# Feed-forward gate and up products with both activation parts in one moving operand

## What is computed

```python
D_FF = ((8 * D_MODEL // 3 + 255) // 256) * 256      # 2816
h = rms_norm(x, w) * (1.0 + scale) + shift
y = (silu(h @ w_gate) * (h @ w_up)) @ w_down        # (256,1024) -> (256,2816) -> (256,1024)
```

## Time and profile before

| | |
|---|---|
| three runs, us | 1251.65, 1252.40, 1252.68; median 1252.4 |
| profiled execution: span, us | 1253.3 (the page gives no other time for it) |
| TensorE busy | 1159.8 us, 93%, 8358 matmuls |
| weight loads busy | 1050.5 us, 84% |
| DVE busy | 932.8 us, 74% |
| ACT busy | 589.0 us, 47% |
| GpSimd busy | 74.6 us, 6% |
| chain that ended last | PE 71%, DVE 17%, ACT 5%, DMA 5% |

### The profile page before, as it was taken

One profiled execution on the slowest core, in us unless ns is written; L12 is line 12 of the kernel. 1 busy time (PEld: TensorE's weight loads), 2 busy tenths in 40 slices (PEclk: granted clock), 3 DMA queues, 4 the chain that ended last, 5 costly groups with the idle time before them and its releaser, 6 DMA issues.

```text
span 1253.3 us, 19977 instructions
## 1 busy us (share of the span) xinstructions
PE 1159.8 (93%) x8358; PEld 1050.5 (84%) x8358; DVE 932.8 (74%) x1630; ACT 589.0 (47%) x968; POOL 74.6 (6%) x106
## 2 busy tenths in 40 slices
PE   2798888999998998899999989999989989999996
PEld 1677568899897996799999979999979967999996
DVE  5967868888786976788978688886765867765445
ACT  1534665344355457544444564444443355444433
POOL 0000000000000000097000000000000000000000
PEclk8799899999999999999999999999999998999998
DMA  9991434788884771467889537789722552765730
GB/s 375 360 371 51 172 135 159 306 310 320 273 333 163 298 263 45 151 249 288 307 229 361 212 139 299 301 246 334 275 103 102 110 177 89 267 240 196 185 133 34
DMA packets 40810, 280.83 MB, mean 224 GB/s; under 512 B 4736, under 2 KB 5264, under 8 KB 7952
## 3 DMA queue, kind: packets, MB, share of 16 engines
q1 hardware_dynamic: 37296, 269.27, 59.3%
q0 software_dynamic: 2416, 7.92, 2.1%
q10 hardware_dynamic: 1008, 2.37, 0.6%
HBM read 277.91 MB, written 1.10 MB: 223 GB/s over the span
## 4 chain that ended last, share of the span: by engine, by line
PE 71%; DVE 17%; ACT 5%; DMA 5%; issue 1%; SPq 0%; DVEq 0%; ACTq 0%
PE PS L408 70%; DVE LO L1385 5%; DMA raw<-WS 4%; DVE raw L1375 4%; ACT HI L957 2%; DMA SC<-scratch 1%; DVE TMP L1485 1%; DVE TMP L1450 1%; DVE HLo L1445 1%; DVE SC L1589 1%; PE PS L612 1%; ACT SC L957 1%; ACT SQ L957 1%; ACT HH L957 1%; ACT RS L957 0%
## 5 line engine op out<-in xcount | busy, mean ns | idle before, releaser
L408 PE MATMUL PS<-HH,HI 128*128 128x256 f32 x1748 | 502.4, 287 | 26.1 <-ACT HH L957 22.3
L408 PE MATMUL PS<-HLo,HI 128*128 128x256 f32 x1748 | 503.3, 288 | 0.4 <-DVE HLo L1445 0.3
L408 PE MATMUL PS<-HH,LO 128*128 128x256 f32 x1748 | 499.5, 286 | 0.2 <-issue 0.2
L1385 DVE TENSOR_TENSOR LO<-raw,HI 128x1024 fp32r<-128x1024 f32 x340 | 403.9, 1226 | 110.5 <-ACT HI L957 110.5
L957 ACT ACTIVATE HI<-raw 128x1024 fp32r<-128x1024 f32 x340 | 339.7, 1048 | 89.3 <-PE PS L408 57.0
L408 PEld LDWEIGHTS PS<-HH,HI 128*128 128x128 f32 x1748 | 340.3, 195 | 35.5 <-DVE LO L1385 19.6
L408 PEld LDWEIGHTS PS<-HH,LO 128*128 128x128 f32 x1748 | 340.4, 195 | 3.4 <-issue 0.5
L408 PEld LDWEIGHTS PS<-HLo,HI 128*128 128x128 f32 x1748 | 339.6, 194 | 3.6 <-DVE HLo L1445 2.2
L1375 DVE CUSTOM_DVE_ANT_0 raw<-raw,CB,SM 128x1024 f32<-128x1024 f32 x168 | 210.4, 1284 | 23.3 <-DMA raw<-WS 23.3
L408 PE MATMUL PS<-HI,HDH 128*128 128x512 f32 x352 | 140.2, 398 | 0.0
L408 PE MATMUL PS<-HI,HDL 128*128 128x512 f32 x352 | 139.5, 396 | 0.0
(11 more groups left out here) (235 smaller groups left out, 1023.6 us busy)
## 6 DMA issues: line engine op xcount, KB each, us to landing
raw<-WS SPq DMA_DIRECT2D x255, 1024.0 KB, 5.4
SC<-scratch POOLq DMA_DIRECT2D x2, 1024.0 KB, 13.3
FB<-gates_out POOLq DMA_DIRECT2D x3, 512.0 KB, 4.9
SQ<-gates_out POOLq DMA_DIRECT2D x3, 512.0 KB, 9.9
X<-xT ACTq DMA_DIRECT2D x1, 1024.0 KB, 7.0
SC<-ssm POOLq DMA_DIRECT2D x2, 512.0 KB, 4.3
out<-TMP SPq DMA_DIRECT2D x2, 512.0 KB, 2.6
CB<-vecs SPq DMA_DIRECT2D x1, 512.0 KB, 6.6
```

Of the source, the lines that this page charges most:

```text
L408: return e.matmul(o, l, r, start=start, stop=stop, skip_group_check=True)
L1385: e.tensor_tensor(LO[:, s % HL, :], raw_half(j, h), HI[:, s % HL, :].bitcast(fp32), O.subtract).then_inc(*D.up(("lo", s)))
```

## The change

HH and HLo become the two halves of one tile HB. From j = 1 on, one matmul of 512 columns gives the high weight's product with HH in columns 0 to 255 and with HLo in columns 256 to 511 of a bank, and one matmul of 256 columns adds the low weight's product with HH to columns 0 to 255. The gate and the up half each have a bank of their own. ACT copies columns 256 to 511 of the gate bank into SIL, DVE adds columns 0 to 255, ACT applies Silu in SBUF. ACT copies the up bank's columns 256 to 511 into HF, DVE adds the other half, and the product is made from HF and SIL in SBUF. Block j = 0 keeps three matmuls of 256 columns, since HLo comes step by step there, but with the new layout.

```diff
--- before.py
+++ after.py
@@ -219,8 +219,8 @@
         X = sb("X", [128, 2, 1024])
         TMP = sb("TMP", [128, 8, 256])
         SQ = sb("SQ", [128, 8, 256])
-        HH = sb("HH", [128, 8, 256], f32r)
-        HLo = sb("HLo", [128, 8, 256], f32r)
+        HB = sb("HB", [128, 2, 8, 256], f32r)
+        HH, HLo = HB[:, 0], HB[:, 1]
         nones = sb("nones", [128, 128])
         zeros = sb("zeros", [128, 128])
         zb = zeros[:, :].bitcast(mybir.dt.bfloat16)
@@ -557,7 +557,7 @@
 
                 for j in range(22):
                     key = (tag, "in", j)
-                    ps = take((key, 0))
+                    pair = [take((key, g)) for g in range(2)]
                     wt = [[x.rearrange("p (k n) -> p k n", k=8) for x in weight(key, 0)]]
                     if j == 0:
                         wt.append([x.rearrange("p (k n) -> p k n", k=8) for x in weight(key, 1)])
@@ -567,15 +567,24 @@
                     for g, k in turns:
                         if len(wt) == g:
                             wt.append([x.rearrange("p (k n) -> p k n", k=8) for x in weight(key, 1)])
-                        i = mm3(ps[:, g * 256:(g + 1) * 256], [x[:, k, :] for x in wt[g]], H2[k], k,
-                                g == 0 and k == 0, k == 7, tag)
+                        ps, high, low = pair[g], wt[g][0][:, k, :], wt[g][1][:, k, :]
+                        w.wait_ge(*A.at(("hh", tag, k)))
+                        if j == 0:
+                            mm(ps[:, 0:256], high, HH[:, k, :], k == 0, False)
+                            mm(ps[:, 0:256], low, HH[:, k, :], False, k == 7)
+                            w.wait_ge(*D.at(("hlo", tag, k)))
+                            i = mm(ps[:, 256:512], high, HLo[:, k, :], False, k == 7)
+                        else:
+                            mm(ps.rearrange("p (c n) -> p c n", c=2), high, HB[:, :, k, :], k == 0, k == 7)
+                            i = mm(ps[:, 0:256], low, HH[:, k, :], False, k == 7)
                         if k == 7:
-                            i.then_inc(*P.up(("in", tag, j), used(key, g)))
+                            i.then_inc(*P.up(("in", tag, j, g), used(key, g)))
                     walk.catch_up(walk.unit - 1, 1)
                     slow(j)
                     if j == 12:
                         mods(gcol + 8)
-                    banks.give((key, 0))
+                    for g in range(2):
+                        banks.give((key, g))
                     if j > 1:
                         down(j - 2)
                 key = (tag, "dn", 10)
@@ -1070,9 +1079,13 @@
                         high(walk.mods(gcol + 8))
                     slow(j)
                     if j > 1:
-                        w.wait_ge(*D.at(("hf", tag, j - 2)))
-                    w.wait_ge(*P.at(("in", tag, j)))
-                    fn(SIL[:, j % 2, :], bank((key, 0))[:, 0:256], F.Silu).then_inc(*A.up(("sil", tag, j)))
+                        w.wait_ge(*D.at(("hdl", tag, j - 2)))
+                    w.wait_ge(*P.at(("in", tag, j, 0)))
+                    fn(SIL[:, j % 2, :], bank((key, 0))[:, 256:512], F.Copy).then_inc(*A.up(("part", tag, j, 0)))
+                    w.wait_ge(*D.at(("sum", tag, j, 0)))
+                    fn(SIL[:, j % 2, :], SIL[:, j % 2, :], F.Silu).then_inc(*A.up(("sil", tag, j)))
+                    w.wait_ge(*P.at(("in", tag, j, 1)))
+                    fn(HF[:, j % 2, :], bank((key, 1))[:, 256:512], F.Copy).then_inc(*A.up(("part", tag, j, 1)))
                     if j == 21:
                         e.preload_act_table_set(LNEXP)
                     w.wait_ge(*D.at(("hf", tag, j)))
@@ -1542,9 +1555,15 @@
                         mods(row[0] + 8)
                     for _ in range(steps):
                         next(later, None)
+                    for g, o in enumerate((SIL[:, j % 2, :], HF[:, j % 2, :])):
+                        w.wait_ge(*A.at(("part", tag, j, g)))
+                        e.tensor_tensor(o, o, bank((key, g))[:, 0:256], O.add) \
+                            .then_inc(*D.up(("free", (key, g)), ("sum", tag, j, g)))
                     w.wait_ge(*A.at(("sil", tag, j)))
-                    e.tensor_tensor(HF[:, j % 2, :], SIL[:, j % 2, :], bank((key, 0))[:, 256:512], O.mult) \
-                        .then_inc(*D.up(("hf", tag, j), ("free", (key, 0))))
+                    w.wait_ge(*D.now())
+                    e.tensor_tensor(HF[:, j % 2, :], HF[:, j % 2, :], SIL[:, j % 2, :], O.mult) \
+                        .then_inc(*D.up(("hf", tag, j)))
+                    w.wait_ge(*D.now())
                     w.wait_ge(*A.at(("hdh", tag, j)))
                     e.tensor_tensor(HDL[:, j % 3, :], HF[:, j % 2, :], HDH[:, j % 3, :].bitcast(fp32), O.subtract) \
                         .then_inc(*D.up(("hdl", tag, j)))
```

## The result

The changed kernel takes 1328.7 us (median of 4 runs, 1325.8 to 1332.3), the kernel before 1252.1 in the same comparison: 1.061 times as long, 95% interval 1.059 to 1.063. The forecast was 1320, in a range of 1290 to 1346.

A forecast was written before the change was run, and what follows sets the result against it. TensorE was taken to bound f0, f1 and f2, with DVE right behind. 25.8 + 23.5 + 17.9 + 3.3 - 1.7 - 0.7 = +68.1 us took the median from 1252.4 to 1320.5, stated as 1320, range 1290 to 1346.

The forecast's parts named there:

- f0: Feed-forward stage: chains add 29.0 us before in(19), less vanishing waits 2.7 and 0.4 and margin 0.1: 25.8 us.
- f1: Feed-forward stage: chains add 29.0 us before in(19), less vanishing waits 2.1 and 0.85 and margin 2.59: 23.5 us.
- f2 with kk: Feed-forward stage f2: 17.9 us from longer chains before in(19), plus 3.3 us for the late kk bank.
- f3: Feed-forward stage where DVE has 80 us idle: the longer chain adds 0, TensorE's faster matmuls give -1.7 us.
- The chain: ACT and DVE work per block up to HDL: 2.51 us instead of 0.90 after DVE can start, 1.61 us more.
- The waits that vanish: DVE waits in f0, f1 and f2 that a later DVE skips: 2.7+0.4, 2.1+0.85 and 2.2+6.45 us subtracted.
- After in(19): Last blocks of a stage: few or no modulation columns remain, DVE catches up, no delay added or given back.
- The bank of kk: Block 12 of f2: in(12) must wait until ACT empties kk's bank; DVE loses 3.3 us, bounds 0 and 7.
- TensorE's part: Matmuls per block from j = 1: 5.66 us instead of 5.74, gain 0.08; -1.7 us in f3, -0.7 elsewhere.
- DVE's idle time would swallow it: Rival: idle DVE time in f0, f1 and f2 absorbs the sums, TensorE gains 6.7 us: 1246 us, chance 0.04.
- the second copy is not waited for: Rival: ACT copies the up half before DVE's first sum ends, 0.86 us a block: 1280 us, chance 0.09.
- the falls of the clock cost some 23 us: Rival: TensorE's new idle time in three stages lowers its clock, adding 23 us: 1343 us, chance 0.12.

The follow-up runs named there:

- Experiment 5: Kernel before, with three extra DVE sums of 128x256 ahead of the product in every block but the first: 1306.7 us, ratio 1.043.
- experiment 2: Changed kernel with its new chain, but 48 matmuls of 256 columns in every block instead of 16 of 512 and 16 of 256: 1330.5 us, ratio 1.062.
- experiment 4: Changed kernel, but ACT empties the bank of kk in block 11 instead of block 12: 1324.4 us, ratio 1.057.
- experiments 1: Changed kernel's matmuls and bank pairs with the old ACT and DVE chain, low activation product not added: 1251.1 us, ratio 0.998 to the kernel before.
- experiment 3: Changed kernel, but ACT makes both copies before the Silu: 1291.4 us, ratio 1.031 to the kernel before.
- experiment 6: Changed kernel, with ten filler matmuls of 512 columns ahead of in(j) in odd blocks 3 to 19 of f0, f1 and f2: 1333.4 us, ratio 1.065.

## Why the prediction was right

The forecast was +68 us, the medians give +77, and the mechanism stands: DVE was right behind TensorE in three of four stages, and a longer chain there became the time. The steps can be measured at the mark that the sum used, the start of in(19) on TensorE (before: the earlier trace rows). After the change, in f0, f1 and f2:

```profile
391.41 0.77 PE L408 MATMUL PS<-HB,HI 128*128 128x512 f32 x1 [3.44 <-DVE LO L1398]
...
741.12 0.47 PE L408 MATMUL PS<-HB,HI 128*128 128x512 f32 x1 [2.33 <-DVE LO L1398]
...
970.36 0.47 PE L408 MATMUL PS<-HB,HI 128*128 128x512 f32 x1 [1.54 <-DVE LO L1398]
```

Each row of the table is the delay that a stage adds to that of the stages before it, first up to the start of in(19), then from there to the last HDL:

| step | predicted, us | measured, us |
|---|---|---|
| ahead of f0 | 0 | +2.9 |
| f0 | 25.8, then -0.2 | 25.4, then +2.2 |
| f1 | 23.5, then -0.2 | 22.3, then +2.3 |
| f2 with kk | 17.9 + 3.3, then -0.2 | 24.5, then +0.3 |
| f3 | -1.7 | -2.6 |
| sum | 68.1 | 77.3 |

So up to in(19) f0 and f1 came out close, and the 9 us that the forecast lacks are mostly the bank of kk, the ends of f0 and f1 and the start ahead of f0.

- **The chain** was forecast at 1.61 us more and measured 1.71. The waits named for it were the right ones: the second copy behind the Silu (0.76 us idle), the handover between DVE's own instructions. 18 times 0.1 us are 1.8 us a stage that the sum had too little.
- **The waits that vanish** were forecast too small, and that they make up for the 1.8 us is luck. By the table f0 took up 18 x 1.71 - 25.4 = 5.4 us and f1 8.5, where 3.2 and 5.5 were subtracted. The working kept 0.53 us for every wait for HI, 6.9, 8.0 and 8.0 us in f0, f1 and f2; up to in(19) 5.0, 6.0 and 6.7 us are left, most of them 0.45 us each. Experiment 5 took up less than the working subtracted and the change took up more; why they differ stays open.
- **After in(19)** the working had DVE catch up and nothing added. That step was wrong. In f1 DVE stays behind to the end: its first operation of block 21 had waited 3.06 us before and now waits for nothing.

```profile
711.77 0.42 DVE L1546 TENSOR_TENSOR FB<-FB,PS 128x256 f32<-128x256 f32 x1 [3.06 <-ACT FB L957]
...
765.62 0.41 DVE L1560 TENSOR_TENSOR FB<-FB,PS 128x256 f32<-128x256 f32 x1
```

  In f0 TensorE begins in(19) at the lower clock, and 5.6 us up to HDL(21) are at that level, where no wait follows that would cover them. In experiment 2 none of that stretch is at the lower level, and f0 adds 0.1 us there instead of 2.2.
- **The bank of kk** was the term of the sum that was sized most wrongly: 3.3 us forecast, 6.3 measured by experiment 4. The working took ACT's copies as shifted by the longer chain only. In the trace after, the matmuls of kk begin at 893.68 and the copies end at 907.30, 13.6 us later; before it was 826.50 to 835.99, 9.5 us, and I had 9.5 + 1.6. ACT follows DVE, and DVE had fallen back against TensorE. Without kk f2 would have come to about 18.2 us at in(19), for 17.9 forecast.
- **TensorE's part** was forecast at 0.08 us a block and is 0.14, since the matmuls of 256 columns took 0.116 us between those of 512 and not 0.120.
- **Ahead of f0** the changed kernel's profiled execution is 2.9 us later (201.37 instead of 198.49 at the same matmul of the norm), in code that the change does not touch, while experiments 1, 2, 3 and 4 have their HDL(0) within 1 us of the kernel before, and experiment 6 has it as late as the changed kernel (218.4 and 218.8). Between 147 and 169 us the clock was at the lower level for 13.7 us in these two, before for 3.4. I take it for a difference between executions; no experiment tells more.
- **Rivals.** That DVE's idle time would swallow it is refuted by experiment 5. That the second copy is not waited for is refuted by the trace and experiment 3. That the falls of the clock cost some 23 us is refuted by experiment 6, although they did come: 51 us at the lower level in f0 to f2, where there were none between the first and the last HDL before. The Trainium skill's rate of 131 ns for 512 columns ("TensorE: Matmul & The Clock Gate", back-to-back issue gap) is not what the trace after shows either: 0.234 us in f3.

Of the signs that were to show an error, one appeared: waits of TensorE for a bank outside block 12 of f2. In(2) waits for DVE's first sum of block 0, 1.9 us in f0 (at 217.93) and 1.2 in f1, and in f1 two waits behind ACT's copies of the product of `slow(j)` take 1.1 us together. In(2) waited for nothing before. So "harmless in plain blocks" did not hold for it; what this costs in the end was not measured. And f3 changed its length by 3.7 us, more than the 3 that were allowed, by the faster matmuls and the later mark.

## What to carry to other kernels

Merging matmuls under one weight load, with the same columns streamed, saved 0.14 us of 5.74 per block here. It pays only where the work that it makes behind TensorE costs less than that or is hidden; here it cost DVE 1.71 us. Before moving an addition from PSUM to a vector engine, look not at that engine's busy share over the span but at its waits in the stage, and count which of them lie inside the chain, because no other work fills those. Where one engine has real rest (f3), the same change pays, and in a queue kept in order the copies that wait for nothing belong ahead of the one that waits.

## What the runs showed of the hardware that was not expected

The second of two DVE sums that follow without a wait starts 0.33 to 0.35 us after the first, though each lasts 0.42 (experiment 3: two in 0.75 us), while a dependent one starts 0.46 us after (243.23 to 243.69). A matmul of 256 columns cost 0.116 us between matmuls of 512 and 0.120 among its like. And a clock that is held high by filling (0.99 instead of 0.96 in f0) gave back 2 us of 200: in a stage that waited for another engine, half speed was nearly free here, except behind the last wait.
